# Dealing anew the fill-in work of the first block: gates and weight pairs alternate, blocks move into the chain of the fourth mixer, the next tile is split earlier

## The reference, cut to what matters

```python
p = _split_in(x @ w_in[l])                       # 25 input blocks of 128 columns (here "in"), and the gates
ya = _mixer_a(p["a_q"], p["a_k"], p["a_v"], ...) # attention with three windows     -> attention "att1", first half
yb = _mixer_b(p["b_q"], p["b_ckv"], p["b_iq"], p["b_ik"], p["b_iw"], ...)
    # score = sum over 8 heads of relu(iq.ik)*iw; top_k(score, 64) keys are kept; attention over these
yc = _mixer_c(...)                               # chunked linear attention, stages c0 to c5
yd = _mixer_d(p["d"], ...)                       # state per head, token by token; here by chunks of 64: "the chain"
    # y = ((y - mean) * rsqrt(var + eps)) * gn_w + gn_b; y = (y + bonus) * g
gates = sigmoid(p["gate"])                       # 4 x 1024 columns: 32 gate tiles
merged = sum_n gates[n] * (ys[n] @ w_branch[n])
x = layer_norm(alpha * x + merged @ w_out)       # then the experts, then the second block
```

## Time and profile before

| | |
|---|---|
| time, median of 3 runs | 1963.24 us (1962.75 to 1963.44) |
| the profiled execution: its own time, its span | 1966.96 us, 1965.2 us |
| mean granted TensorE clock | 0.952 |
| busy: PE, DVE, ACT, POOL | 1773.5, 949.5, 757.8, 100.9 us |
| first block up to the first branch products | about 0 to 410 us of the span |
| ring tiles issued in the first 480 us | 175, of 512 KB, median 5.5 us from issue to landing |

### The profile page before, as it was taken

The page is one execution under the profiler, slowest core; times in us unless marked ns, Lnnn a source line. Parts: engine busy times, 40 slices in busy tenths (PEclk is TensorE's granted clock), DMA queues, the critical chain, the costliest instruction groups (busy, mean ns, idle before and its releaser), DMA issues.

```text
span 1965.2 us, 32818 instructions
## 1 busy us (share of the span) xinstructions
PE 1773.5 (90%) x12838; PEld 1366.5 (70%) x12838; DVE 949.5 (48%) x1741; ACT 757.8 (39%) x1399; POOL 100.9 (5%) x158
## 2 busy tenths in 40 slices
PE   6888779987799999899999899999998799989997
PEld 6775657776444444487778588788876686789997
DVE  4742543377622211427344655435535454568684
ACT  5331323453122111423564533323335334555454
POOL 0010000004000000100000200000002000010000
PEclk8998889997899999999999899999998899989999
DMA  5598546766288889722101123222321230135552
GB/s 222 174 238 304 173 174 226 262 209 182 108 330 317 332 314 344 271 78 77 39 1 44 54 92 101 86 97 86 103 87 58 86 108 1 48 123 185 182 181 77
DMA packets 84850, 303.43 MB, mean 154 GB/s; under 512 B 10144, under 2 KB 12192, under 8 KB 84576
## 3 DMA queue, kind: packets, MB, share of 16 engines
q1 hardware_dynamic: 80640, 290.49, 42.8%
q0 software_dynamic: 2736, 7.35, 1.6%
q10 hardware_dynamic: 1328, 3.55, 0.5%
HBM read 347.22 MB, written 3.15 MB: 178 GB/s over the span
## 4 chain that ended last, share of the span: by engine, by line
PE 75%; DMA 11%; DVE 8%; ACT 4%; issue 2%; SPq 0%; ACTq 0%; DVEq 0%
PE bank L888 47%; PE bank L833 17%; DMA ring<-wall 10%; PE bank L1351 3%; PE bank L912 2%; PE bank L1389 2%; PE bank L1364 2%; PE bank L1374 2%; DVE w_lo L2028 1%; ACT w_hi L1581 1%; DVE BIG L2640 1%; DMA con<-consts 1%; PE bank L1411 0%; ACT XC L1650 0%; ACT BIG L1642 0%
## 5 line engine op out<-in xcount | busy, mean ns | idle before, releaser
L888 PE MATMUL bank<-BIG_f32r,w_hi 128*128 128x256 f32 (+1 forms) x2208 | 552.6, 339 | 23.6 <-DVE BIG_f32r L2043 15.6
L2028 DVE TENSOR_TENSOR w_lo<-ring,w_hi 128x1024 fp32r<-128x1024 f32 x260 | 322.6, 1250 | 352.5 <-ACT w_hi L1581 351.2
L888 PEld LDWEIGHTS bank<-BIG_f32r,w_hi 128*128 128x128 f32 x2208 | 382.8, 192 | 73.5 <-issue 25.5
L888 PE MATMUL bank<-BIG_f32r,w_lo 128*128 128x256 f32 (+1 forms) x1136 | 387.6, 341 | 0.0
L1581 ACT ACTIVATE w_hi<-ring 128x1024 fp32r<-128x1024 f32 x260 | 271.5, 1053 | 246.5 <-PE bank L888 157.1
L888 PE MATMUL bank<-AR_f32r,w_hi 128*128 128x256 f32 (+1 forms) x1066 | 268.7, 331 | 16.7 <-issue 9.4
L888 PEld LDWEIGHTS bank<-BIG_f32r,w_lo 128*128 128x128 f32 x1136 | 217.2, 191 | 25.4 <-issue 0.2
L888 PEld LDWEIGHTS bank<-AR_f32r,w_hi 128*128 128x128 f32 x1066 | 186.1, 193 | 37.6 <-issue 9.9
L888 PE MATMUL bank<-AR_f32r,w_lo 128*128 128x256 f32 (+1 forms) x448 | 147.5, 329 | 0.0
L888 PE MATMUL bank<-lnst_f32r,w_hi 128*128 128x256 f32 x318 | 101.2, 318 | 36.6 <-DVE w_lo L2028 33.4
L888 PE MATMUL bank<-XC_f32r,w_lo 128*128 128x256 f32 x424 | 127.6, 301 | 0.0
(11 more groups left out here) (357 smaller groups left out, 2294.4 us busy)
## 6 DMA issues: line engine op xcount, KB each, us to landing
ring<-wall SPq DMA_DIRECT2D x546, 512.0 KB, 4.6
w_extra<-wall SPq DMA_DIRECT2D x96, 512.0 KB
BIG<-t_rows POOLq DMA_DIRECT2D x16, 128.0 KB, 13.4
AR<-na_rows POOLq DMA_DIRECT2D x32, 64.0 KB, 7.4
con<-consts ACTq DMA_DIRECT2D x1, 1810.0 KB, 12.0
na_rows<-rpb_pad POOLq DMA_DIRECT2D x1, 1792.0 KB, 32.5
XC<-xin ACTq DMA_DIRECT2D x1, 1024.0 KB, 6.4
XC<-ctxin POOLq DMA_DIRECT2D x1, 1024.0 KB, 6.4
```

The costliest lines, as they stand in the source:

```text
L888: ins = nc.tensor.matmul(o, l, r, start=start and n == 0, stop=stop and n == 2, **kw)
L2028: V.tensor_tensor(w_lo[:, i % SPLIT_RING, :], ring[:, t % RING, :], w_hi[:, i % SPLIT_RING, :].bitcast(F32), ALU.subtract).then_inc(w_spli ...
```

## The change

The sum of work is the same: the same products, copies, splits and DMAs. What changes is the table, the rule for how far ahead tiles are split, and the place of three pieces of DVE work.

- Table: `feat` and `split` get 3 pairs instead of 2; `split` keeps one input block instead of two, and the later blocks move back by one to three points. ak1, cv0 with cv1, and av0 with av1 move from before the chain into chunks 0, 1 and 2 (points X0, X1, X2). The pairs that stood in X, U and Yc of the chunks now stand in U and M, and the rest of them before the chain. In att0 to att4, gates and pairs alternate. c3, c4 and c5 are dealt anew: one gate each in c3 and c4, the last three gates in c5 with two pairs between each.
- Rule: before a block's result is copied out, ACT and DVE feed its own tile, the next tile of the same point, and the split tile behind its own also where that lies less than 6 tiles behind the point's first one (`split_next`, `split_through`). At the end of each point they feed up to two more (`split_ahead`); in the attention this stands at the end of the step.
- DVE: the end of the fourth mixer becomes `d_finish()`, called in step 0 after the maxima; `choose` is dealt 1, 3, 3, 1 over steps 0 to 3 instead of 2, 2, 2, 2.

```diff
 BESIDE = {
...
-    "feat": ins_("iq0", "iq1", "ik", "ckv") + ada_(2),
-    "split": ins_("bq0", "bq1") + ada_(2),
-    "Z1": ins_("cq") + ada_(1),
+    "feat": ins_("iq0", "iq1", "ik", "ckv") + ada_(3),
+    "split": ins_("bq0") + ada_(3),
+    "Z1": ins_("bq1") + ada_(1),
...
-    "chain": ins_("ak1", "av0"),
+    "chain": ins_("ak0"),
+    "X0": ins_("ak1"), "U0": ada_(1), "M0": ada_(1),
+    "X1": ins_("cv0"), "U1": ada_(1), "M1": ada_(1),
+    "X2": ins_("av0"), "U2": ada_(1), "M2": ada_(1),
+    "X3": ada_(1), "U3": ada_(1), "M3": [],
...
-    BESIDE[f"att{_t}"] = ada_(2 if _t < 5 else 1) + gates_(6 - _t // 2, 2 * (_t % 2), 2 * (_t % 2) + 1)
+    _g = gates_(6 - _t // 2, 2 * (_t % 2), 2 * (_t % 2) + 1)
+    BESIDE[f"att{_t}"] = ada_(1) + _g[:1] + ada_(1 if _t < 5 else 0) + _g[1:]
...
-BESIDE["c5"] = gates_(0, 2, 3) + ada_(2)
+BESIDE["c5"] = gates_(0, 1) + ada_(2) + gates_(0, 2) + ada_(2) + gates_(0, 3)
...
+    def split_through(unit):
+        return split_at[early[unit[-1]]] + 1
+
+    def split_next(point, unit):
+        n = split_through(unit)
+        return n + (1 if split_order[n] < min(first_of[point] + RING, moe0) else 0)
+
+    def split_ahead(point):
+        n = sum(t <= last_of[point] for t in split_order)
+        end = n
+        while end < n + 2 and split_order[end] <= min(first_of[point] + RING + 2, last_of[point] + RING, moe0 - 1):
+            end += 1
+        return end
...
-            def beside(point):
-                for work_ in BESIDE[point]:
-                    if work_[0] == "in":
-                        feed_in(work_[1])
-                    elif work_[0] == "gate":
-                        feed("gate", 4 * work_[1] + work_[2])
+            def beside(point, ahead=True):
+                for unit in split_items(point):
+                    feed_to(split_next(point, unit))
+                if ahead:
+                    feed_to(split_ahead(point))
...
                     if st == "att1":
-                        beside(f"att{t}")
-                        if t < 4:
-                            choose(2 * t)
-                            choose(2 * t + 1)
+                        beside(f"att{t}", ahead=False)
+                        if t == 0:
+                            d_finish()
+                        for k in ((0,), (1, 2, 3), (4, 5, 6), (7,))[t] if t < 4 else ():
+                            choose(k)
                         if t == 3:
                             select()
+                        feed_to(split_ahead(f"att{t}"))
```

More of the change, by code:

```diff
@@ L93 @@
     "kk": ins_("dk1", "dv0", "dv1"),
-    "feat": ins_("iq0", "iq1", "ik", "ckv") + ada_(2),
-    "split": ins_("bq0", "bq1") + ada_(2),
-    "Z1": ins_("cq") + ada_(1),
+    "feat": ins_("iq0", "iq1", "ik", "ckv") + ada_(3),
+    "split": ins_("bq0") + ada_(3),
+    "Z1": ins_("bq1") + ada_(1),
     "D4": ada_(1),
-    "Z2": ins_("ck") + ada_(1),
-    "Z3": ins_("cv0"),
+    "Z2": ins_("cq") + ada_(1),
+    "Z3": ins_("ck") + ada_(1),
     "Pm": ins_("cg0") + ada_(1),
-    "P2t": ins_("cg1", "aq0"),
-    "Y1": ins_("aq1") + ada_(1),
-    "T": ins_("ak0"),
-    "chain": ins_("ak1", "av0"),
-}
-for _c in range(NCH):
-    for _w in ("X", "U", "Yc"):
-        BESIDE[f"{_w}{_c}"] = ada_(1)
-BESIDE["var"] = gates_(7, 0, 1)
-BESIDE["std"] = ada_(2) + gates_(7, 2, 3)
+    "P2t": ins_("cg1") + ada_(1),
+    "Y1": ins_("aq0") + ada_(1),
+    "T": ins_("aq1") + ada_(1),
+    "chain": ins_("ak0"),
[3 more added lines that the diff above has]
+    "X3": ada_(1), "U3": ada_(1), "M3": [],
+    "var": gates_(7, 0, 1),
+    "std": gates_(7, 2) + ada_(2) + gates_(7, 3),
+}
 for _t in range(8):
-    BESIDE[f"att{_t}"] = ada_(2 if _t < 5 else 1) + gates_(6 - _t // 2, 2 * (_t % 2), 2 * (_t % 2) + 1)
+    _g = gates_(6 - _t // 2, 2 * (_t % 2), 2 * (_t % 2) + 1)
+    BESIDE[f"att{_t}"] = ada_(1) + _g[:1] + ada_(1 if _t < 5 else 0) + _g[1:]
 for _t in range(8, 11):
@@ L115, with split_items @@
 BESIDE["c0"] = gates_(2, 3) + ada_(1)
-BESIDE["c1"] = gates_(1, 0, 1) + ada_(2)
+BESIDE["c1"] = gates_(1, 0) + ada_(2) + gates_(1, 1)
 BESIDE["c2"] = gates_(1, 2) + ada_(1)
-BESIDE["c3"] = gates_(1, 3) + ada_(1)
-BESIDE["c4"] = gates_(0, 0, 1) + ada_(2)
-BESIDE["c5"] = gates_(0, 2, 3) + ada_(2)
+BESIDE["c3"] = gates_(1, 3)
+BESIDE["c4"] = gates_(0, 0)
+BESIDE["c5"] = gates_(0, 1) + ada_(2) + gates_(0, 2) + ada_(2) + gates_(0, 3)
+def split_items(point):
+    units = []
+    for w in BESIDE[point]:
+        if w[0] == "in":
+            units.append([("in", IN_BLOCKS.index(n)) for n in (w[1], IN_PAIRS.get(w[1])) if n])
+        elif w[0] == "gate":
+            units.append([("gate", 4 * w[1] + w[2])])
+    return units
 R_W, R_A, R_G, R_C = 0, 32, 64, 96
@@ L587, in build @@
             for what in ("X", "U", "Yc", "M"):
-                if what == "M" and c == NCH - 1:
-                    continue
-                add((what, c, 0), (what, c, 1))
+                if what != "M" or c < NCH - 1:
+                    add((what, c, 0), (what, c, 1))
+                if what != "Yc":
+                    add_beside(f"{what}{c}")
         add(*[("ix", 0, q) for q in range(4)], "ymean")
@@ L1701, in _ @@
             ada_pairs_seen = [0]
-            def beside(point):
+            def beside(point, ahead=True):
+                units, at = split_items(point), 0
                 for work_ in BESIDE[point]:
+                    if work_[0] != "ada":
+                        feed_to(max(split_next(point, units[at]), split_through(units[min(at + 1, len(units) - 1)])))
+                        at += 1
                     if work_[0] == "in":
-                        in_unit(work_[1])
+                        for n in (work_[1], IN_PAIRS.get(work_[1])):
+                            if n:
+                                in_out(n)
                     elif work_[0] == "gate":
                         _, m, n = work_
-                        feed("gate", 4 * m + n)
                         if m == 4:
@@ L1796, in _ @@
                     beside(f"{what}{c}")
-                beside(f"Yc{c}")
+                beside(f"M{c}")
             def index_relu(i, qs):
@@ L2287, in _ @@
                           (what, c, 0))
+                    beside(f"{what}{c}")
                 for p in range(2):
@@ L2356, in _, with d_finish @@
             beside("std")
-            dve.wait_ge(sem("d_std"), 1)
-            step(V.reciprocal(DD["e1"], DD["e1"]))
-            step(V.tensor_tensor(yT, yT, DD["e1"], ALU.mult))
-            for m in range(2):
-                step(V.tensor_scalar(yT[:, m, :], yT[:, m, :], p_("d_gn_w")[:, m:m + 1], p_("d_gn_b")[:, m:m + 1],
-                                     ALU.mult, ALU.add))
-            step(V.tensor_tensor(yT, yT, bn, ALU.add))
-            evacuated(dve, "dg")
-            step(V.tensor_tensor(ysT[:, 3, :, :], yT, DZ["g"], ALU.mult), "d_out")
+            def d_finish():
+                dve.wait_ge(sem("d_std"), 1)
+                step(V.reciprocal(DD["e1"], DD["e1"]))
+                step(V.tensor_tensor(yT, yT, DD["e1"], ALU.mult))
+                for m in range(2):
+                    step(V.tensor_scalar(yT[:, m, :], yT[:, m, :], p_("d_gn_w")[:, m:m + 1], p_("d_gn_b")[:, m:m + 1],
+                                         ALU.mult, ALU.add))
+                step(V.tensor_tensor(yT, yT, bn, ALU.add))
+                evacuated(dve, "dg")
+                step(V.tensor_tensor(ysT[:, 3, :, :], yT, DZ["g"], ALU.mult), "d_out")
             attention("att1")
```

13 lines of the change are left out of this document (11 added, 2 removed).

## The result

The changed kernel is slower: 1972.24 us median (1969.46 to 1975.44, 6 runs) against 1963.22 (1960.31 to 1964.20, 6 runs) for the kernel before, ratio 1.0053 with a 95% interval of 1.0039 to 1.0067. The forecast was 1951.0. The profiled execution took 1971.75 us, its span is 1970.0; the one before had 1966.96. So the two profiled executions differ by 4.8 us where the medians differ by 9.0: the one before was taken 3.7 us above its median, and what the traces give is good to some microseconds only.

A forecast was written before the change was run, and what follows sets the result against it. After the first block PE was taken as busy nearly throughout, so only its waits were followed. +16.4 - 21.4 - 2.8 - 4.5 = -12.3 us took the profiled 1966.96 to 1954.7, median 1951.0, range 1933 to 1966.

The forecast's parts named there:

- Term A: 64 us to the end of the chain: the change adds waits, +16.4 us, bounds +2 to +25.
- Term D: `c4` and `c5`: PE's waits fall from 6.8 to 2.3 us, -4.5 us, bounds -1 and -6.8.
- D8 then waits 2.6 for the adds, as it did before: Before the chain, behind the wait for `ckvms`: PE waits 2.6 us for DVE's adds, unchanged.
- P2t, Y1 and T: Points behind D8, with 10 to 13.5 us to landing: PE waits 1.0, 3.3 and 2.4 us.
- the 20.4: Sum of PE's forecast waits ahead of the chain, 20.4 us against 12.1 before: +8.3 us.
- the -1.0 of the pair in `feat`: In `feat` the third pair fills 1.0 of the 2.5 us that PE waits for L2235: -1.0 us.
- bq1: End of `split`: ACT and DVE wait for t24, in the slot of a tile read just before; +2.3 us.
- bq0: Could start at 77.0 but finds no tile until 80.4, as s11 is split only behind the masks: +3.4 us.
- U3: In the chain: t69 and t70 take slots of M2's own pair, so U3 waits 7.1 us.
- Term B: `var` to the scores of step 4: waits of 27.3 us fall to 10.4, clock gives 4.5; -21.4 us, bounds -26 and -11.
- Term C: Steps 4 and 5: two waits of 1.4 us go, -2.8 us, bounds 0 and -2.8.
- Rival 1: Look-ahead blocks: landing stays 13.5 us in the chain, Term A +41, kernel slower at 1975.5 us; chance 0.10.

The follow-up runs named there:

- e13_pool_late: Changed kernel with POOL's 16 bias DMAs started only at T and its 1.8 MB copy only behind yvar; ratio 1.0045 to the kernel before.
- e9_z2: Changed kernel without the look-ahead at the end of Z2; ratio 1.0061 to the kernel before, median 1974.01 us.
- e1_mid: Kernel before with only var to att10 as in the changed kernel; ratio 0.9917 to the kernel before.
- e10: e1_mid with `d_finish` again ahead of step 0 of the attention and `choose` dealt 2-2-2-2; ratio 0.9940 to the kernel before.
- e11: e1_mid with the old split rule also from var to att10; ratio 0.9936 to the kernel before.
- e14: e12 with the new split rule in c0 to c5, on the old table there; ratio 0.9870 to the kernel before.
- e15: e12 with the new table in c0 to c5, under the old split rule there; ratio 0.9895 to the kernel before.
- e17: e12 with the new split rule in c4 and c5 alone, on the old table; ratio 0.9830 to the kernel before, median 1929.45 us.
- e12: e1_mid with g70 and g71 split behind the last Yc, and the splits of `var` behind the scores; ratio 0.9879 to the kernel before.

## Why the prediction was wrong

The mechanism that the text named as the danger is the one that made the kernel slower; its size was put too low in A, and in D it wasn't looked for.

- **Term A, +27.4 instead of +16.4: the step that failed.** It is "D8 then waits 2.6 for the adds, as it did before": it waits 10.05 us, 7.5 more. It did not wait 2.6 before either, but 3.5. The text had the ring's landing at 10 to 13.5 us for what comes behind D8, and applied it at P2t, Y1 and T, but not to the look-ahead at Z2, whose tile t35 lands 10.5 us after its issue. e13_pool_late shows that 4.4 of the 10.05 are POOL's traffic, and in e9_z2, without that look-ahead, 0.3 is left at D8, though the next look-ahead takes the wait over. Against that Pm, P2t, Y1 and T together came out smaller (1.6 and 2.0 us, where 6.7 were put), and so did the waits in the chain (11.9 for 13.9).
- **Where the rest of A went.** I count from the first product of the families to the mean, with the windows view of that stretch, before and after:

```profile
64.24:194.36 130.12, 115.55 (x1572) 88.23 (x1572) 57.02 (x95) 35.93 (x60) 10.01 (x18) 0.92 0.79 247
63.53:221.72 158.19, 119.85 (x1575) 92.12 (x1576) 59.19 (x97) 38.64 (x63) 10.01 (x18) 0.87 0.68 215
```

- The stretch grew by 28.1 us: PE's idle time by 23.8 (14.6 to 38.3) and its busy time by 4.3, with the same products. The granted clock fell from 0.95 to 0.91 in the families and from 0.86 to 0.80 in the chain, where after the change four of eight pairs took about 1.93 us instead of 1.06. The text gave B a term for the clock and A none, although A adds the gaps. Its own terms for this stretch come to +19.9, not +16.4, as the 20.4 stand against all 12.1 of the old waits, of which the 2.5 for L2235 lie ahead of the stretch (1.8 still stand there after the change), as does the -1.0 of the pair in `feat`. So of the 11.7 us between 28.1 and 16.4, 4.3 are clock, 3.9 idle time, 2.5 the dropped wait and 1.0 that pair.
- **Single waits that were right.** bq1 2.2 (put at 2.3), `ckvms` 5.8 (5.4), bq0 3.2 (3.4), X1's 2.6 (3.3), U3 6.3 (7.1): the rows for a landing, a split and a pair give such a wait to within 1 us. At U0 they did not: 2.2 where 1.1 was put. By the figure of the Trainium skill (DMA: Bandwidth & Descriptors, Anatomy of one DMA, about 2 us fixed) U3 would have waited 5.0; the 6.3 lie between it and the 7.1 by the trace's median. (The section gives that figure for DMAs that GpSimd issues; here SP issues them. Both tiles that U3 waits for landed after 4.7 and 4.9 us.)
- **Term B, -21.5, forecast -21.4.** Right in sum and in the main members: yvar 4.1 (4.1), g62 2.2 (2.4), `select` gone. That the sum comes out to 0.1 is partly luck: g72 waited for nothing (2.5 was put) and steps 1 and 2 for 0.3 (1.4), so that the idle time fell by 20.0 instead of 16.9, while the busy time fell by only 1.5 where 4.5 were put for the clock (0.86 to 0.91 granted). e1_mid shows the part alone, -16 by its ratio and -21 at step 5 in its trace. That the order of the maxima and the look-ahead carry 4 to 8 us each, and the alternation the rest, is what e10 and e11 suggest; it is not shown, as no run had the alternation alone.
- **Term C, -3.0, forecast -2.8**: right; no run tests it by itself.
- **Term D, +4.8 instead of -4.5** (+4.2 as a mean over the traces of all kernels). The text costed c4 and c5 alone and took c0 to c3 as unchanged, though the rule acts in every point. In this trace PE's idle time there grew by 2.8 us and its busy time by 1.9, at a granted clock of 0.87 instead of 0.91 up to `coms`. PE waited 1.6, 1.9 and 1.8 us for g11, g12 and `c_states` (L2456), where it had waited 0.8 in all, and behind `coms` the 2.7 for g03 (2.3 was put) are joined by 1.4 for the tiles of the pairs. e14 and e15 suggest that neither table nor rule alone does it; e17 beside e12 shows that the rule in c4 and c5 alone, on the old table, gains: 7.5 us in the trace, 9.6 by the ratios. So what failed in D is that c0 to c3 were taken as unchanged; why both together cost what neither did alone stays open.
- **The rivals and the numbers.** Rival 1 put its threshold at A = +28.7 with the other terms as forecast; A came to +27.4, with which the other terms as forecast would have given -1.3 in all; D, +4.8 instead of -4.5, made it slower. The rival's reason, landings of 13.5 us in the chain, did not hold: the 20 tiles issued between 172 and 218 us landed after 4.3 us in the median, and the waits there came to 11.9 us in sum where 13.9 were forecast. The chance of 0.10 for slower was too small, and the bounds of +2 to +25 on A did not hold the +27.4: the high one took a long landing only at M2, none at Z2, and no term for the clock.

## What to carry over

A split (or any prefetch step) that waits for a landing on an engine with a fixed order is a wait for everything behind it: put it where the slot was freed a whole landing ago, or behind the last copy that another engine needs. Read the landing time from the stretch in which the tile will be issued, with the other queues' DMAs in it, and do so at every point that the rule touches, not only at the one that it was written for. When a change has parts that lie in different stretches, run them apart: here one part gave -16 us and another +30.
